# NSA attention: the second head's transposed probabilities are copied out of PSUM by VectorE instead of ScalarE

## The reference, cut to what matters

```python
pc = _masked_softmax(jnp.einsum('bqgrd,bcgd->bqgrc', qb, kcmp) * scale, mask_c)
o_cmp = jnp.einsum('bqgrc,bcgd->bqgrd', pc, vcmp)
...
ps = _masked_softmax(ss, mask_s).reshape(b, NSA_QBLOCK, G, R, SEL_TOPK, SEL_BLOCK)
o_slc = jnp.einsum('bqgrkl,bgqkld->bqgrd', ps, v_g)
...
pw = _masked_softmax(jnp.einsum('bqgrd,bkgd->bqgrk', qb, kwb) * scale, mask_w)
o_win = jnp.einsum('bqgrk,bkgd->bqgrd', pw, vwb)
return gb[..., 0:1] * o_cmp + gb[..., 1:2] * o_slc + gb[..., 2:3] * o_win
```

## Time and profile before

| | |
|---|---|
| median of 3 runs | 2164.83 us (2163.47 to 2165.17) |
| profiled execution | 2163.54 us, its span 2161.6 us |
| share of the span busy | PE 92%, DVE 48%, ACT 26%, POOL 3% |
| NSA attention, first scores to last output copy | 440.62 to 494.93 us of the span |

### The profile page before, as it was taken

How to read it: one execution, slowest core, us unless ns; L and a number is a source line. 1 busy time by engine, 2 the same in 40 slices (tenths; PEclk the granted TensorE clock), 3 DMA queues, 4 the chain that set the end, 5 groups by cost and what they waited for, 6 DMA issues and landing times.

```text
span 2161.6 us, 27523 instructions
## 1 busy us (share of the span) xinstructions
PE 1984.5 (92%) x9979; PEld 1386.0 (64%) x9979; DVE 1042.7 (48%) x2206; ACT 565.2 (26%) x1176; POOL 59.4 (3%) x68
## 2 busy tenths in 40 slices
PE   6999898889889999979899899999999788999997
PEld 4888687657745555544355388888444355778886
DVE  3456662377332222235666877676787224423311
ACT  3333300171121111131174133332000124433410
POOL 0000000000000000000000001010000010000000
PEclk9999999989999999989899999999999888999999
DMA  9355382414559999530102312222674011134451
GB/s 389 140 208 216 142 335 88 161 55 193 210 199 426 425 424 419 219 136 0 39 1 103 131 61 95 78 96 112 265 264 176 0 55 47 40 117 153 144 203 44
DMA packets 39464, 357.25 MB, mean 165 GB/s; under 512 B 4295, under 2 KB 9038, under 8 KB 10318
## 3 DMA queue, kind: packets, MB, share of 16 engines
q1 hardware_dynamic: 39374, 356.04, 42.1%
HBM read 354.97 MB, written 1.05 MB: 165 GB/s over the span
## 4 chain that ended last, share of the span: by engine, by line
PE 86%; DVE 5%; ACT 2%; DMA 2%; issue 2%; DVEq 1%; PEldq 1%; PEld 1%; SPq 0%; ACTq 0%
PE bank L643 47%; PE bank L1299 12%; PE bank L1106 6%; PE bank L1091 3%; PE bank L1128 3%; PE bank L748 2%; PE bank L669 2%; PE bank L1271 2%; PE bank L1194 1%; DMA ring<-in_ada 1%; PE bank L1201 1%; ACT hn L1378 1%; DVE rstd L1834 1%; PE bank L1067 1%; DVE ring L1935 1%
## 5 line engine op out<-in xcount | busy, mean ns | idle before, releaser
L643 PE MATMUL bank<-hn,ring 128*128 128x256 f32 (+1 forms) x2080 | 520.4, 410 | 13.6 <-ACT hn L1378 9.7
L643 PE MATMUL bank<-arena,ring 128*128 128x256 f32 (+2 forms) x1600 | 470.4, 452 | 25.1 <-issue 13.1
L643 PEld LDWEIGHTS bank<-hn,ring 128*128 128x128 f32 x2080 | 399.1, 193 | 123.0 <-issue 67.8
L643 PEld LDWEIGHTS bank<-arena,ring 128*128 128x128 f32 (+1 forms) x1600 | 300.8, 190 | 190.8 <-issue 154.1
L1299 PE MATMUL bank<-hn,ring 128*128 128x256 f32 x704 | 161.0, 382 | 6.2 <-ACT hn L1378 6.2
L1299 PEld LDWEIGHTS bank<-hn,ring 128*128 128x128 f32 x704 | 134.6, 191 | 25.6 <-issue 7.0
L1814 DVE SCALAR_TENSOR_TENSOR bank<-ring,c_rows 128x1024 f32<-128x1024 f32 x96 | 118.1, 1230 | 34.2 <-DMA ring<-in_ada 29.2
L1299 PE MATMUL bank<-ring 128*128 128x256 f32 x528 | 122.9, 383 | 3.2 <-DVEq L2535 3.2
L1366 ACT ACTIVATE hn<-resid 128x256 f32<-128x256 f32 (+1 forms) x64 | 30.0, 492 | 349.8 <-DVE resid L1893 341.9
L1814 DVE SCALAR_TENSOR_TENSOR ring<-ring,c_rows 128x1024 f32<-128x1024 f32 x96 | 117.2, 1220 | 0.0
L1299 PEld LDWEIGHTS bank<-ring 128*128 128x128 f32 x528 | 100.9, 192 | 18.5 <-issue 3.9
(11 more groups left out here) (382 smaller groups left out, 2165.1 us busy)
## 6 DMA issues: line engine op xcount, KB each, us to landing
ring<-in_ada SPq DMA_DIRECT2D x28, 2048.0 KB, 8.2
ring<-in_up SPq DMA_DIRECT2D x44, 1024.0 KB, 4.9
ring<-in_egu SPq DMA_DIRECT2D x20, 2048.0 KB, 11.6
ring<-in_edn SPq DMA_DIRECT2D x39, 1024.0 KB, 10.2
ring<-in_down SPq DMA_DIRECT2D x16, 1408.0 KB, 9.5
arena<-in_egu SPq DMA_DIRECT2D x10, 2048.0 KB, 11.4
hn<-in_egu SPq DMA_DIRECT2D x9, 2048.0 KB, 11.6
ring<-in_adat SPq DMA_DIRECT2D x8, 2048.0 KB, 12.7
```

Of the source, the lines that this page charges most:

```text
L643: last = mm(out, lhs(i), rhs(i), start=i == 0, stop=i == k - 1)
```

## The change

In this attention alone, head 1's copy (item 6, e = 1) moves from ACT to DVE. ACT keeps head 0's copy and now adds 2 to `att_PT`, so that later attentions count on as before. A new semaphore, `att_PT_second`, is counted up by DVE's copy. PE's transposes of head 1 wait for it before they overwrite bank 5, and PE's values wait for both. DVE's copy stands in step p behind the scalings of pair p-1 and copies pair p-2.

```diff
                         for e in range(2):
-                            if t >= 1:
+                            if t >= 1 and masked and e == 1:
+                                pe.wait_ge(s["att_PT_second"], t)
+                            elif t >= 1 and masked:
+                                pe.wait_ge(s["att_PT"], 2 * t)
+                            elif t >= 1:
                                 pe.wait_ge(s["att_PT"], 2 * (done + t) + (e - 1))
...
                         pe.wait_ge(s["att_PT"], 2 * (done + v + 1))
+                        if masked:
+                            pe.wait_ge(s["att_PT_second"], v + 1)
...
-                        for e in range(2):
+                        for e in range(1 if pairs[t].branches == 2 else 2):
                             act_e.wait_ge(s["att_T"], 2 * (done + t) + (e + 1))
-                            fn(probs_t[t % 2][:, e, 0:w], banks[:, 4 + e, 0:w], ACT.Copy).then_inc(s["att_PT"], 1)
+                            fn(probs_t[t % 2][:, e, 0:w], banks[:, 4 + e, 0:w], ACT.Copy).then_inc(s["att_PT"], pairs[t].branches)
...
                         last.then_inc(s["att_scaled"], 1)
+                    if 2 <= p < N + 2 and pairs[p - 2].branches == 2:
+                        t = p - 2
+                        w = 2 * pairs[t].w
+                        ve.wait_ge(s["att_T"], 2 * (done + t + 1))
+                        if t >= 2:
+                            ve.wait_ge(s["att_O"], done + t - 1)
+                        V.tensor_copy(probs_t[t % 2][:, 1, 0:w], banks[:, 5, 0:w]).then_inc(s["att_PT_second"], 1)
```

More of the change, by code:

```diff
@@ L275, in build @@
             cs_mm cs_max cs_exp cs_ready ct_mm ct_ev
-            att_S att_max att_exp att_scaled att_T att_PT att_O att_ev
+            att_PT_second att_S att_max att_exp att_scaled att_T att_PT att_O att_ev
             route_pe route_dve route_act tok_mm tok_ev
```

## The result

The changed kernel takes 2169.17 us (median of 17 runs, 2166.55 to 2175.77), the kernel before 2164.83 (17 runs): a ratio of 1.0024, 95% interval 1.0016 to 1.0031. It is slower by 4 to 5 us, twice the 2.0 that I had summed. A second set of both gave 2168.91 against 2165.40, 1.0012 (1.0003 to 1.0021).

What follows compares the result with a forecast made beforehand. Three engines were near full in the attention, with DVE's and PE's lines tying after the change. Five periods at 0.39 us more, all else at nothing, gave +2.0 us on the median 2164.83: 2166.8, range 2164.2 to 2170.0.

Steps and rivals of the forecast that it cites:

- The period: One odd and one even attention step from step 5 on: 5.96 us would become 6.35, 0.39 more, five times.
- TensorE's route behind the wide copy: From DVE's 512-column copy through head 1's transposes, values and next scores to DVE's next masks: 6.34 us per period.
- DVE's own line: DVE's instructions of one period, start to start: 5.38 us without the new copies, 6.33 us with them.
- the early steps: Attention steps before step 5, at clock 0.85: DVE's waits for PE of 0.91 and 0.44 us absorb the new copies.
- the tail: Last pair's two copies at the attention's end, able to run on two engines at once: nothing gained back.
- The shift passes on whole: Behind the attention: all engines meet at its end, so everything later moves by the same amount, about 2 us.
- the clock's term: PE's granted clock in the attention would stay at 1.00; a drop, another +3.7 us, was held unlikely and not summed.
- The rival that I had dismissed: PE's lower busy share, about 90%, lowers its clock in the attention: another +3.7 us, counted within the slower case's 0.15.
- within 0.2%: Whole kernel: the time differs by at most 4.3 us from before; chance 0.81.
- hidden: DVE's idle time in the attention swallows the copies: 0 to +1.2 us, 2164.8 to 2166.0; chance 0.15.
- TensorE's restart: PE restarts late after the new wait, period up by 1.11 us: +8.9 us, 2173.7; slower case's chance 0.15.
- Not ACT: Rival that ACT's exponentials set the attention's loop, so fewer ACT copies make it faster: 2159 to 2160.5; chance 0.04.

Runs made afterwards that it cites:

- wide_only: Changed kernel with only the 512-column pairs' head 1 copies on DVE, the 256-column ones on ACT; 2171.05 us against 2165.40 before, ratio 1.0027.
- output_first: Changed kernel with DVE's output copy put ahead of the wide copy in the odd step; 2169.01 us against 2165.10 before, ratio 1.0019.
- after_again: Changed kernel run and traced once more, code unchanged; 2168.91 us against 2165.40 before, ratio 1.0012.
- pad_08: Kernel before, no copy moved, with 8 more repeated PE transposes of the last pair's head 0; 2168.56 us against 2164.84, ratio 1.0015.
- pad_16: Kernel before, no copy moved, with 16 more repeated PE transposes of the last pair's head 0; 2169.44 us against 2164.84, ratio 1.0019.
- filled: Changed kernel with PE doing head 0's two transposes of each narrow pair twice, inside its wait; 2171.96 us against 2165.10 before, ratio 1.0029.
- narrow_only: Changed kernel with only the 256-column pairs' head 1 copies on DVE, the 512-column ones on ACT; 2165.89 us against 2165.40 before, ratio 1.0002.
- The paddings: Kernels with 8, 16 or 32 more last-pair transposes on the kernel before, or 14 more on the changed kernel; ratios 1.0015, 1.0019, 1.0017, 1.0019.
- split_scores_first: Kernel before with DVE signalling scalings per head and PE's next scores ahead of the values; 2161.38 us against 2165.78, ratio 0.9981.

## Why the prediction was wrong

**What held.** The period: 6.35 us predicted, 6.33 measured. Its cause: TensorE's route behind the wide copy, tied with DVE's own line, which wide_only and output_first separate. The answer to the copy within 0.06 us. The price of the copies to the next start, 0.60 and 0.35 us for 0.61 and 0.34. In after_again the early steps, whose waits swallow their copies (in the first trace they ran at half clock, 10.23 us for 6.69); the tail, of which nothing came back; ACT, which gained idle time (0.79 us before a wide copy and more before the exponentials) and set nothing. The stage's +1.85 us in after_again and the +1.8 and +2.4 at equal clock stand beside the predicted +2.0. The estimate from the overhead that the Trainium skill's page "Perfetto Trace Analysis" gives (section "Optimizing Scalar/DVE Operations") was 658 and 392 ns for the two copies; the trace has 0.68 and 0.42 us as lengths, and the estimate's sum, +2.4 us, is no worse than mine by these runs.

**The step that failed** is "The shift passes on whole", with the clock's term put at nothing in the sum. I had taken what stands behind the stage as stiff: 2 us later, and else the same. It is the same program, but not the same clock. The mean clock falls from 0.9635 to 0.9616 and 0.9627, and at 1.24 us for each 0.001 that is 2.4 and 1.0 us on top. Together with the level at equal clock they make +4.8 and +2.8 us, which is the means of the two sets less before's mean of 2165.3; the fit splits that difference so, and the agreement is no proof of the split. What stands by itself is the stage's +1.85 us in after_again's trace and the lower clock of pad_08 and pad_16, in which no copy is moved. So the term that I had put at nothing measured about as much as my whole sum in the first set and half of it in the second. Two kinds of place are seen where it was paid: 1.69 us behind the pause at 555 us, in half the traces; and the attention itself, in two of the seven traces with wide copies moved and TensorE's order kept (60.54 us in the first trace, 59.51 in wide_only's, for 56.43).

**The rival that I had dismissed** came near: I named the clock, but looked for it only inside the stage, tied it to TensorE's busy share there, and gave it a part of 0.15. In the first trace some 4 us were lost inside the stage, near the +3.7 that I had named and held for unlikely, though in its early steps, with TensorE busy all the time, and so not for the reason I gave. The share was indeed enough: at 1.00 the clock stayed 1.00 in all full periods with TensorE busy 5.93 of 6.33 us. filled raised the share and got no clock back. The chance for "within 0.2%" was too high for another reason too: a sum of +2.0 us beside a bound of 4.3 left room for one such extra only.

**The other rivals.** Not hidden (narrow_only is, at +0.1; the wide copies are not). Not TensorE's restart, 0.06 us. Not ACT.

**What stays open.** Why one execution meets a lower clock and another not, and whether the start time alone decides it, is not in the traces. Nor is whether moved copies make the losses inside the stage more frequent: the paddings change nothing before the stage's last transposes and can't test it. The Trainium skill's page "TensorE: Matmul & The Clock Gate", Part 1, says that what the gate watches runs free and doesn't start anew with a kernel. The paddings agree with that, but no run here shows it directly. Nor is it settled how much of the +2.9 and +3.0 at equal clock of wide_only and filled, some 0.8 over the changed kernel's, is work and how much a low clock where TensorE is full, which costs more than the common slope. wide_only's one trace has such a stretch, 6.82 us at 0.50 at the stage's end; filled's stage took 56.76 us in its trace and has none (it has 8 x 0.21 us of work more, most of it inside a wait).

## What to carry to other kernels

When an engine's copy frees the buffer that the head of another engine's queue waits for, follow that queue to what it feeds: here a copy of 0.69 us on DVE cost because PE's next scores stood behind it, and reordering the scores took the cost away where freeing DVE would not have. Before moving work to the less busy engine, look for the loop that sets the period; opening it (split_scores_first) gave 0.19% where moving the copies lost 0.24%. And a difference of a few microseconds in a kernel with many pauses needs the mean clock beside it: compare at equal clock, or pad by two or three lengths, before a cause is named. Here eleven executions left the mean clock uncertain by 0.0003 to 0.0005, which is 0.4 to 0.6 us.

## What the runs showed of the hardware that was not expected

- 0.86 us of additional work of TensorE made the kernel 3.7 us slower at the median, and 3.4 us of it 4.5 us. What the clock cost did not rise with what was added.
- At 0.50, 1.2 GHz, TensorE was busy for 10.23 of 10.23 us and stayed there; in other executions the same matmuls at the same place were at 1.00 after a part of that time. The Trainium skill's "Perfetto Trace Analysis", section "Matmul Optimizations", has the engine scale its power with its utilization and asks for matmuls back to back; the full stretch at 0.50 and filled's 0.9609 show that being busy alone decided neither the rise of the clock nor the time here.
- The clock fell to 0.50 with the longest idle times of TensorE just before it at 1.88 us (behind the pause, after_again) and 1.09 us (wide_only's end of the stage), and in other executions it stayed at 1.00 behind the same pause.
- The same pause of 1.9 us is followed by 32 matmuls in 7.17 us or in 8.86, and executions of one kernel differ by up to 9 us (2166.55 to 2175.77), with 0.964 and 0.958 as mean clocks.
- DVE's copy of 512 columns out of PSUM took 0.68 to 0.69 us beside PE's transposes into the neighbouring bank and ACT's exponentials, as long as elsewhere in the kernel.
